# Decode scores of two sequences: from two 128x64 tiles of the array with zeros in the queries to eight 64x32 tiles with dense queries

## The reference, cut to what matters

```python
full_slc = jnp.concatenate([gather_pages(cache_slc_kv, page_table), kvs_s], axis=1)   # 16 pages of 128 rows, k and v, 2 kv heads x 64
win_ctx = jnp.concatenate([state_win_kv, kvw_s], axis=1)                               # last 512 rows
# in selected_attention and window_attention, per kv head k with its 4 query heads g:
s = jnp.einsum('bkgd,bkmd->bkgm', q, keys) * (HEAD_DIM ** -0.5) - slope * dist         # queries x keys, contraction over 64
p = masked_softmax(s, mask)
o = jnp.einsum('bkgm,bkmd->bkgd', p, values)
```

## Time and profile before

| | us |
|---|---|
| median of 3 runs | 752.14 (752.06 to 753.49) |
| the profiled execution | 753.13 |
| its span in the trace | 751.4 |
| PE busy | 712.4 (95%) |
| DVE, ACT, POOL busy | 268.7, 170.1, 231.6 |
| mean DMA rate | 255 GB/s |

### The profile page before, as it was taken

One profiled execution on the slowest core, in us unless ns is written; L12 is line 12 of the kernel. 1 busy time (PEld: TensorE's weight loads), 2 busy tenths in 40 slices (PEclk: granted clock), 3 DMA queues, 4 the chain that ended last, 5 costly groups with the idle time before them and its releaser, 6 DMA issues.

```text
span 751.4 us, 16367 instructions
## 1 busy us (share of the span) xinstructions
PE 712.4 (95%) x6460; PEld 401.1 (53%) x6460; DVE 268.7 (36%) x724; ACT 170.1 (23%) x366; POOL 231.6 (31%) x393
## 2 busy tenths in 40 slices
PE   6999999999989887988999998999999999999998
PEld 3555456865766554666645544454445555445542
DVE  1200054068678768566222366110011110001147
ACT  3100030248456644333010121000101000110100
POOL 2465156898575647444000001000000000000050
PEclk9999999999999899999999999999999999999999
DMA  9966523069801998467995065699999999999874
GB/s 300 262 174 230 173 50 71 20 198 226 228 20 40 323 310 266 134 180 211 241 415 223 29 265 182 241 321 358 399 419 425 419 422 420 424 413 420 352 270 137
DMA packets 81938, 191.79 MB, mean 255 GB/s; under 512 B 15798, under 2 KB 54982, under 8 KB 77373
## 3 DMA queue, kind: packets, MB, share of 16 engines
q1 hardware_dynamic: 67461, 150.63, 56.0%
q0 software_dynamic: 12160, 31.97, 13.0%
q10 hardware_dynamic: 2240, 8.13, 2.7%
HBM read 174.09 MB, written 16.70 MB: 254 GB/s over the span
## 4 chain that ended last, share of the span: by engine, by line
PE 53%; DVE 8%; issue 3%; DMA 2%; ACT 1%; SPq 1%; POOL 0%; DVEq 0%; POOLq 0%; ACTq 0%
PE bank L1353 31%; PE bank L1254 7%; PE bank L1337 2%; DVE arena L2011 2%; PE bank L1200 1%; PE bank L1445 1%; PE bank L1283 1%; PE bank L1274 1%; PE bank L1245 1%; DMA arena<-in_w_out 1%; DMA arena<-expert_rows,row_i 1%; DVE arena L2021 1%; DVE arena L2014 1%; PE bank L1379 1%; PE bank L1106 1%
## 5 line engine op out<-in xcount | busy, mean ns | idle before, releaser
L1353 PE MATMUL bank<-arena,proj 128*32 128x256 f32 (+1 forms) x2352 | 237.0, 479 | 1.3 <-DVE proj L2229 0.8
L1353 PEld LDWEIGHTS bank<-arena,proj 128*32 128x32 f32 x2352 | 103.3, 110 | 94.7 <-issue 76.3
L2424 POOL DMA_INDIRECT proj<-normed_rows,idx x12 | 11.4, 953 | 302.6 <-PE bank L1337 190.7
L909 PE MATMUL bank<-arena,amT 128*128 128x454 f32 x256 | 101.8, 556 | 1.1 <-DMA arena<-in_w_in 1.1
L2239 DVE TENSOR_TENSOR proj<-proj,bank 128x256 f32<-128x256 f32 x24 | 10.0, 421 | 208.1 <-PE bank L1353 208.1
L2334 POOL DMA_DIRECT2D arena<-in_cache_cmp_kv x128 | 68.6, 536 | 50.3 <-issue 42.6
L909 PEld LDWEIGHTS bank<-arena,amT 128*128 128x128 f32 x256 | 48.9, 194 | 50.0 <-issue 49.9
L2341 POOL DMA_DIRECT2D arena<-in_cache_slc_kv x96 | 51.5, 536 | 42.0 <-PE bank L1203 17.7
L1353 PE MATMUL bank<-amT,proj 128*32 128x512 f32 (+1 forms) x336 | 56.5, 532 | 0.0
L1353 PE MATMUL bank<-queries_and_bias,proj 128*32 128x512 f32 (+1 forms) x384 | 56.5, 486 | 0.0
L2354 POOL COPY arena<-arena 128x268 f32<-128x268 f32 x64 | 37.8, 647 | 27.9 <-PE bank L906 20.3
(11 more groups left out here) (358 smaller groups left out, 1011.9 us busy)
## 6 DMA issues: line engine op xcount, KB each, us to landing
arena<-in_w_up SPq DMA_DIRECT2D x13, 2048.0 KB, 16.5
arena<-in_w_down SPq DMA_DIRECT2D x13, 2048.0 KB, 16.6
arena<-in_w_gate SPq DMA_DIRECT2D x10, 2048.0 KB, 17.1
arena<-in_cache_cmp_kv POOLq DMA_DIRECT2D x128, 64.0 KB, 2.5
arena<-in_cache_cmp_kv SPq DMA_DIRECT2D x128, 64.0 KB, 2.2
amT<-in_w_gate SPq DMA_DIRECT2D x3, 2048.0 KB, 12.8
queries_and_bias<-in_w_gate SPq DMA_DIRECT2D x3, 2048.0 KB, 11.6
expert_rows<-proj ACTq DMA_DIRECT2D x11, 512.0 KB, 9.7
```

The costliest lines, as they stand in the source:

```text
L909: last = pe.matmul(ps(("in", c, i))[0:n, 0:WC], xnT[:, k, i * P:i * P + n], w_in[c % 2][:, k, :], start=k == 0, stop=k == KC - 1)
L1353: ins = pe.matmul(dst[part, :], rows[:, part], own if q < TRIO else shared, start=start, stop=stop)
```

## The change

The scores of two sequences are taken on eight 64x32 tiles of the array. Each (sequence, kv head) pair has 32 of the 128 columns; the upper and the lower 64 rows of the array hold the same queries and stream different keys. So the 16 pages of a sequence are treated as two halves: the matmuls of the upper rows score one half of the pages, those of the lower rows the other half, into two PSUM banks (`slc_s(t, n, half)`). For that each half needs the keys of head h in the right 64 rows. The keys of pages 0 to 7 are turned as before ("even" spans, x = 0: head 0 above, head 1 below). The keys of pages 8 to 15 are turned in spans shifted by 64 columns (x = 1: head 1 of page k above, head 0 of page k + 1 below), for which keys and values now lie in separate areas of the page buffer; the last span of a sequence takes two transposes. `queries_of_sample` writes the queries twice (upper and lower rows) without zeros, and the memset of `QB` is gone.

Also changed: there are two score groups of eight matmuls in a round instead of four of two, and the window keys are turned between them. All eight banks of keys are turned ahead of the first group, into eight key buffers instead of four. Scores of the new keys and of the window are four matmuls each on 64x32 tiles, all in one bank. On DVE the four mask passes (L2126 after, L2014 before) and the minimum over them are moved from between the copies to the end of the round, behind the copies of the turned probabilities; on ACT the two exponentials go to the end of the round too, the window's first. The compressed branch's decode scores use the same tiles. The block mask is laid out in ten small operations instead of one. A load of keys and values of a page (sequences 0 to 3) writes two pieces of 512 bytes per token instead of one of 1 KB.

```diff
@@ s_scores(t), PE
-                for c in range(5):
-                    if c < 4:
-                        for s in range(2):
...
-                            for k in range(4):
-                                last = pe.transpose(ps(name)[:, k * P:(k + 1) * P], pages[b % 4][:, 4 * c + k, 0:P], ident)
-                            written(last, name)
-                    if c:
-                        name = ("slc_s", t, c - 1)
...
-                        for s in range(2):
-                            q = slice(64 * s, 64 * s + 64)
-                            last = pe.matmul(ps(name)[q, :], QB[:, 2 * t + s, q], kb[(10 * t + 2 * (c - 1) + s) % 4], start=True, stop=True)
-                        written(last, name)
+                def turn_page(dst, b, k, shifted):
+
+                    keys = page_keys[b % 4]
+                    if not shifted:
+                        return pe.transpose(dst, keys[:, k * P:(k + 1) * P], ident)
+                    if k < HALF_PAGES - 1:
+                        c = (HALF_PAGES + k) * P + HD
+                        return pe.transpose(dst, keys[:, c:c + P], ident)
+                    pe.transpose(dst, keys[:, HALF_PAGES * P - HD:HALF_PAGES * P + HD], ident)
+                    return pe.transpose(dst[0:HD, :], keys[:, PAGES * P - HD:PAGES * P], ident)
...
+                def scores(n):
+
+                    names = [("slc_s", t, n, half) for half in range(2)]
...
+                    for s in range(2):
+                        for h in range(KVH):
+                            q = rows_of(s, h)
+                            for half in range(2):
+                                rows = slice(64 * half, 64 * half + 64)
+                                last = pe.matmul(ps(names[half])[q, :], QS[rows, t, q], key_buffer(t, 4 * n + 2 * s + (h ^ half))[rows, :],
+                                                 start=True, stop=True)
...
+                def scores_of(name, keys_at, n):
+
+                    opened(pe, name)
+                    for s in range(2):
+                        for h in range(KVH):
+                            rows, q = slice(64 * h, 64 * h + 64), rows_of(s, h)
+                            last = pe.matmul(ps(name)[q, 0:n], QS[rows, t, q], keys_at(s)[rows, :], start=True, stop=True)
+                    written(last, name)
+
+                for n in range(2):
+                    keys(n)
+                scores(0)
                 for s in range(2):
                     b = 2 * t + s
                     pe.wait_ge(ld_win_state[b % 4], 16 * (b // 4 + 1))
...
+                scores(1)
...
+                scores_of(("win_s", t), lambda s: key_buffer(t, 8 + s), 512)
+                scores_of(("new_s", t), lambda s: kTs[:, SEQ:NT], NS)
+                scores_of(("neww_s", t), lambda s: kTw[:, SEQ:NT], NS)
@@ memory
-        kb = [view(arena, 2 * SW + 2 * WW + i * 512, 512) for i in range(4)]
+        kb = [view(arena, 2 * SW + 2 * WW + i * 512, 512) for i in range(4)] + [proj[:, 3, 0:512], proj[:, 4, 0:512], kTs[:, 0:512], kTw[:, 0:512]]
@@ page loads, SP and POOL alike
-                    sp.dma_start(pages[b % 4][:, k, first * P:(first + count) * P], src)\
+                    sp.dma_start(pages[b % 4][:, first:first + count, k, :], src)\
@@ scalar engine, end of the round (taken from behind the key copies)
+                if t < PAIRS:
+                    d = 72 + 2 * (t % 2)
+                    sc.wait_ge(w_z, t + 1)
+                    sc.activation(SN[t % 2], SN[t % 2], ACT.Exp, ...)
+                    sc.wait_ge(s_z, t + 1)
+                    sc.activation(S[t % 2], S[t % 2], ACT.Exp, ...)
@@ vector engine, end of the round (taken from between the key copies)
+                if t < PAIRS:
+                    for n, half in ((0, 0), (0, 1), (1, 0), (1, 1)):
+
+                        c = 2 * half + n
+                        taken(ve, ("slc_s", t, n, half))
+                        z3 = Sb[:, c * 512:(c + 1) * 512].rearrange("p (n l) -> p n l", l=64)
+                        last = ve.tensor_tensor_reduce(z3, z3, bc(maskb[:, t, 8 * c:8 * c + 8], 64), -1.0, 3e38, ALU.add, ALU.min,
+                                                       st[:, 84 + c:85 + c])
+                    link(last)
+                    taken(ve, ("new_s", t))
+                    ve.tensor_reduce(st[:, 80:81], st[:, 84:89], X, ALU.min).then_inc(s_z, 1)
```

More of the change, by code:

```diff
@@ L23 @@
 NPAGES = DB * PAGES
+HALF_PAGES = PAGES // 2
 NBS = PAST // 64
@@ L1138, in s_scores @@
[L1138 to L1143 removed]
+                    for s in range(2):
+                        for x in range(2):
+                            taken(pe, ("slc_k", t, n, s, x))
+                    for s in range(2):
+                        for h in range(KVH):
+                            q = rows_of(s, h)
+                            for half in range(2):
+                                rows = slice(64 * half, 64 * half + 64)
+                                last = pe.matmul(ps(names[half])[q, :], QS[rows, t, q], key_buffer(t, 4 * n + 2 * s + (h ^ half))[rows, :],
+                                                 start=True, stop=True)
+                                if s == h == 1:
+                                    written(last, names[half])
```

209 lines of the change are left out of this document (107 added, 102 removed).

## The result

The changed kernel takes 745.46 us (median of 5 runs, 744.33 to 750.3), the kernel before 752.14: a ratio of 0.9917 with an interval of 0.9896 to 0.9938. It is faster, by 6.7 us of the medians where some 9 were forecast (743.0), and inside the stated range of 739 to 748.5. Two later measurements of the same kernel on other chips gave 0.9937 (0.9914 to 0.9961) and 0.9943 (0.9921 to 0.9965), a gain of 5.3 and 4.3 us by the medians.

A forecast was written before the change was run, and what follows sets the result against it. PE was taken as busy nearly everywhere, alternating with DVE in decode rounds; 4.0 + 2.7 + 2.7 - 0.2 = 9.2 us off the profiled 753.1 gives 743.9, or 743.0 for the median, range 739 to 748.5.

The forecast's parts named there:

- PE's scores: Decode rounds: eight tiles take about the 1.01 us of a former pair; the window group takes 0.85, at most 1.7.
- Rounds 0 and 1: Compressed branch starts 5.5 us earlier, less 1.5 us for a low clock behind PE's stop: 4.0 us saved.
- The stop: Round 1: PE stands 5.2 us, from 286.2 to 291.4, behind round 0's moved masks, minimum and long exponential.
- Rounds 2 and 3: Each shrinks from 21.17 to 18.5 us, as masks and most of the long exponential lie beside the values: 2.7 saved each.
- land 6.1 us into the round: Rounds 2 and 3: second sequence's window rows land then, while PE wants them at 5.3, a new wait of 0.8 us.
- The wait for DVE's last copy: Rounds 2 and 3: PE waits 1.7 us for the probabilities' copies before the values start at 13.1.
- The clock in rounds 2 and 3: Part of a rival: the clock falls again at the 1.7 us waits, costing 1.2 us in each round; rival's chance 0.14.
- The tail, the split pages, the memset and the 16 copies: Decode's end, loads of sequences 0 to 3, the memset and copies beside busy PE: each forecast to cost 0.
- The tail's forecast of 11.8 us: From the end of round 2's `slc_o` to the projection's first product; a later start would show the prediction wrong.
- rivals of the tiles: Eight tiles and window tiles don't stream together: 0.85 us per unhidden group, 5.1 in all, giving 748.1; chance 0.13.
- of the late pages: Split pages come late at PE's first turn of round 1, through POOL's descriptor work: 753 to 757 us; chance 0.04.
- that of the low clock: Clock low through round 1 (2.9 us instead of 1.5) and again in rounds 2 and 3: 746.8; chance 0.14.

The follow-up runs named there:

- k_all: Changed kernel plus window values first, half the output weights early, round 0's masks and exponential put off, window rows of sequences 4 and 5 early: 745.83 us, ratio 0.984.
- a_third: The changed kernel unaltered, measured a third time: 754.16 us against 758.47 for the kernel before, ratio 0.9943.
- b_masks0: Changed kernel with round 0's four mask passes, minimum and long exponential put off into round 1: ratio 0.9894 to the kernel before.
- d_wincopy: Changed kernel with DVE's copy of the second window's keys behind the second distance pass instead of ahead: ratio 0.9919 to the kernel before.
- all with rows 4 to 7 early: Window values first, half the output weights early, round 0's masks put off, window rows of sequences 4 to 7 asked for early: 742.24 us against 752.94, 0.9853.

## Why the prediction was right, and where it was not

- **PE's scores** were right: 1.02 us for a group of eight, 0.86 for the window group, and 8.06 us for all of round 0's turns and scores against 7.9. The upper bound of 1.7 was never reached. The Trainium skill ("TensorEngine Tiling (Array Packing)", Gotcha 1: PSUM Pressure) says that different row tiles cannot access one bank at the same time; the 0.86 us show no cost of that here, where the tiles write different partitions of the bank.
- **Rounds 0 and 1** were right in mechanism and nearly in size: 4.3 to 4.4 us saved against 4.0. The stop was 4.05 us instead of 5.2: counted from the first key turn, the turns of round 1 ended 0.6 us later than forecast (they ran without a wait for a bank), and the stop ended 0.6 us earlier. The clock cost what was said: from the first scores to the compressed branch 5.71 us, and 4.26 at full clock in k_all, so 1.45 against 1.5. The run with the masks put off shows that cause: the stop shrinks to 0.52 us and the clock stays at 1.00 behind it.
- **Rounds 2 and 3** hold the mis-sized term: 2.7 us each were forecast, and round 2 saved 2.2, 3.0 and 3.0 in the three profiles, round 3 only 1.0, 1.5 and 0.3. The step that failed is that the window rows "land 6.1 us into the round" with a wait of 0.8. PE turned the second row at 6.9, 6.1 and 6.0 us in round 2, but at 7.9, 7.4 and 7.6 us in round 3. The prediction took the landing times of the kernel before, 5.6 and 5.5 us for the second row. In round 2 they hold (6.2, 5.4 and 5.3 us), in round 3 it takes 7.3, 6.7 and 6.9. Sharing the engines with the value pages makes 0.3 to 1.2 us of it in round 2 (values held back); why round 3's rows take 1.1 to 1.6 us more than round 2's stays open. That the late rows are what round 3 lost is shown by the window values first: with the rows in time it takes 16.35 us. The wait for DVE's last copy, forecast at 1.7 us, was 1.2.
- **The clock in rounds 2 and 3**, a rival's part: behind the wait of 2.04 us of the third profile the granted clock fell to 0.61 in 336 to 340, and round 3 took 20.4 us; behind 2.38 us in the first it did not. Of eight profiles with waits of 1.7 to 2.4 us in this place three show it (a_third, b_masks0, d_wincopy); what decides is not shown.
- **The tail, the split pages, the memset and the 16 copies** cost nothing that the runs can tell. The tail's forecast of 11.8 us is counted wrongly: in the earlier trace rows it is 11.5 us from the end of `slc_o` to the projection, as the prediction says elsewhere, and 11.85 from the start of its last four matmuls. After, the same two are 11.65 and 12.04, so the tail grew by 0.2 us, and by the second count the projection starts 0.2 us behind the 11.8 that the prediction named as a sign of being wrong. POOL's sixteen issues of sequence 3 grew from 9.4 to 11.3 us, far from doubled, and PE's first turn of round 1 waits for no DMA.
- **The remainder.** The decode is 7.3, 8.9 and 7.4 us shorter in the profiles, and the runs are 6.7, 5.3 and 4.3 us faster by the medians. The prediction let the rest of the program only shift. It did not: in each of the three profiles the projection and router stage takes 102.3 us instead of 100.57, and its last twelve instructions hold 1.6 to 1.7 us of that (6.87, 7.01 and 7.01 us instead of 5.32, at a lower granted clock). In b_masks0 and k_all these run at full clock, and the stage takes 100.5 us. All runs say the same for the whole: the mean granted clock of a run was 0.986 for the changed kernel on both later chips (6 and 10 runs), against 0.994 and 0.995 for the kernel before (11 and 15 runs). As an estimate from these means and the two levels, some 12 to 13 us more ran at 1.2 GHz, which costs at most some 6 us, of which round 1 is 1.45. So the clock is a term that the sum had only for round 1, and it can account for what is missing. Why the changed kernel draws more of it behind the decode stays open.
- **Luck.** The first measurement, 6.7 us, is the one of three that lies nearest to the forecast; the other two, 5.3 and 4.3, are about half of the forecast, though the decode gained 7.3 to 8.9 us each time. The rivals of the tiles and of the late pages were rightly dismissed; that of the low clock was partly true, in other places than it named.

## What to carry to other kernels

In this kernel, giving PE less to do paid only together with a shorter list on the engine that it alternates with: the tiles and the new order of turns, with masks and exponentials in their old place, made it 1% slower; with them moved behind the values it was 0.6 to 0.8% faster. After such a step, list what each queue issues just ahead of the next load that is now wanted earlier: the row of 16 or 32 page issues ahead of the window rows was worth 2 to 4 us, and to put the small consumer (window values) first freed its buffer 4 us sooner. An end that is bound by a load (the output weights) took back 3 to 4 us of what was gained ahead of it, and behind each such wait (window values first with and without the masks put off, all with rows 4 to 7 early, values held back) the projection began at a granted clock of 0.50 to 0.57, so that projection and router took 1.8 to 3.1 us more than in the kernel before. Such a load has to be moved with the rest. And when a gain measured in one stage doesn't arrive in the total, compare the granted clock of the stages behind it.

## What the runs showed of the hardware

The same instructions behind the same waits (0.35 us before, 0.34 after, ahead of the row of twenty small matmuls) met two clocks. Windows of the router stage, before and after, PE only (busy us, granted clock, DMA share, GB/s):

```profile
454.00:458.00 4.00, 3.65 (x17) 1.00 0.73 311
458.00:462.00 4.00, 4.00 (x19) 1.00 0.16 22
```

```profile
448.00:452.00 4.00, 3.66 (x18) 1.00 0.67 279
452.00:456.00 4.00, 4.00 (x15) 0.61 0.16 20
```

Between chips the program differs by some 8 us, nearly all of it in the last experts, where 128 instructions took 7.09 us in the first profile of the changed kernel and 15.9 in the third, with idle time between them that the profile puts down to "issue", that is, to nothing that it shows:

```profile
719.47 7.09 PE L1402 MATMUL bank<-arena,proj 128*32 128x256 f32 x128
```

```profile
721.84 0.63 PE L1402 MATMUL bank<-arena,proj 128*32 128x256 f32 x3 [0.48 <-issue]
723.26 1.10 PE L1402 MATMUL bank<-arena,proj 128*32 128x256 f32 x4 [0.79 <-issue]
...
727.54 8.28 PE L1402 MATMUL bank<-arena,proj 128*32 128x256 f32 x92 [0.35 <-issue]
```

From the first expert product to the end it was 283 to 286 us in seven profiles and 291 to 294 in seven, and the seven long ones are those of two of the chips. The cause is not shown. The kernel before shows the same in its medians, 752 to 753 us on some chips and 758 to 760 on others.
